# Encoder layer with two attention branches: the banded branch scheduled two pairs per round

## The reference, cut to what matters

```python
def window_attention(q, k, v, rel_bias, sink):       # 8 query heads, 2 key heads, blocks of 128 queries
    logits = einsum(q_block, keys of the block and its two neighbours)
    logits = where(|i - j| <= 128 and inside, logits + bias, -1e30)
    m = maximum(max(logits), sink)
    p = exp(logits - m)
    p = p / (sum(p) + exp(sink - m))
    return einsum(p, v)
...
merged = sigmoid(ga) * oa + sigmoid(gb) * ob
x = x + gt1 * (merged @ w_out)
h2 = rms_norm(x) * (1 + sc2) + sh2
x = x + gt2 * expert_choice_moe(h2)                   # 16 experts, the larger part of the time
```

## Time and profile before

| | us |
|---|---|
| median of 3 runs | 2331.76 |
| lowest and highest | 2330.65, 2332.59 |
| the profiled execution: its own time | 2333.09 |
| the span of its profile | 2331.3 |
| TensorE busy | 2274.2 (98%) |
| VectorE busy | 1622.0 (70%) |
| ScalarE busy | 1223.5 (52%) |
| banded branch: first scores (item 40) to first product of the merge | 431.55 to 540.77 |

### The profile page before, as it was taken

The page is one execution under the profiler, slowest core; times in us unless marked ns, Lnnn a source line. Parts: engine busy times, 40 slices in busy tenths (PEclk is TensorE's granted clock), DMA queues, the critical chain, the costliest instruction groups (busy, mean ns, idle before and its releaser), DMA issues.

```text
span 2331.3 us, 55130 instructions
## 1 busy us (share of the span) xinstructions
PE 2274.2 (98%) x24018; PEld 1663.7 (71%) x24018; DVE 1622.0 (70%) x1977; ACT 1223.5 (52%) x1568; POOL 1089.1 (47%) x707
## 2 busy tenths in 40 slices
PE   7998999999999999989999999999999999999997
PEld 3554677664444458788888888888888888888874
DVE  4776666483222456878887878788878878887875
ACT  4233666583111245457556555665566555665654
POOL 0000111133323214656666677667666766766752
PEclk9999999999999999989999999999999999999998
DMA  9101201503222345578899999989998999999896
GB/s 339 35 28 70 58 2 38 182 2 91 55 55 62 101 146 165 185 271 319 303 333 343 314 335 334 324 314 343 331 320 319 344 331 311 340 334 320 322 326 251
DMA packets 252439, 524.24 MB, mean 225 GB/s; under 512 B 8411, under 2 KB 57676, under 8 KB 252076
## 3 DMA queue, kind: packets, MB, share of 16 engines
q1 hardware_dynamic: 241692, 488.51, 59.4%
q0 software_dynamic: 10512, 32.25, 4.8%
HBM read 492.42 MB, written 28.31 MB: 223 GB/s over the span
## 4 chain that ended last, share of the span: by engine, by line
PE 90%; DVE 3%; ACT 2%; DMA 2%; issue 1%; SPq 1%; POOL 0%; DVEq 0%; POOLq 0%; ACTq 0%
PE ps L1870 24%; PE ps L1871 24%; PE ps L1872 24%; PE ps L2265 4%; PE ps L2054 3%; PE ps L2066 3%; PE ps L1931 3%; PE ps L1966 1%; DMA arena<-w_in 1%; PE ps L2004 1%; ACT arena L1085 1%; PE ps L1907 1%; PE ps L2238 1%; PE ps L1956 1%; PE ps L2202 1%
## 5 line engine op out<-in xcount | busy, mean ns | idle before, releaser
L1870 PE MATMUL ps<-arena 128*128 128x160 bf16 (+4 forms) x5624 | 1391.9, 267 | 6.9 <-issue 2.7
L1871 PE MATMUL ps<-arena 128*128 128x160 bf16 (+4 forms) x5624 | 1392.5, 267 | 0.0
L1872 PE MATMUL ps<-arena 128*128 128x160 bf16 (+4 forms) x5624 | 1392.4, 267 | 0.0
L1392 DVE TENSOR_TENSOR arena<-arena 128x2048 bf16<-128x2048 f32 x379 | 912.1, 2411 | 217.9 <-ACT arena L972 212.7
L972 ACT ACTIVATE arena<-arena 128x2048 bf16<-128x2048 f32 x384 | 727.0, 1905 | 217.9 <-PE ps L1872 176.2
L1870 PEld LDWEIGHTS ps<-arena 128*128 128x128 bf16 x5624 | 550.2, 98 | 157.6 <-issue 18.3
L1872 PEld LDWEIGHTS ps<-arena 128*128 128x128 bf16 x5624 | 550.2, 98 | 152.3
L1871 PEld LDWEIGHTS ps<-arena 128*128 128x128 bf16 x5624 | 550.2, 98 | 140.6 <-issue 0.3
L868 POOL TENSOR_TENSOR arena<-arena 128x320 bf16<-128x320 f32 x128 | 260.3, 2034 | 10.0
L865 POOL TENSOR_TENSOR arena<-arena,ones 128x320 bf16<-128x320 f32 x128 | 193.2, 1510 | 138.9 <-DVE arena L1735 138.6
L1243 ACT ACTIVATE arena<-ps 128x160 f32<-128x160 f32 x256 | 77.6, 303 | 299.8 <-PE ps L1872 299.8
(11 more groups left out here) (267 smaller groups left out, 2211.1 us busy)
## 6 DMA issues: line engine op xcount, KB each, us to landing
arena<-w_e_gate SPq DMA_DIRECT2D x64, 2048.0 KB, 8.9
arena<-w_e_up SPq DMA_DIRECT2D x64, 2048.0 KB, 9.8
arena<-w_e_down SPq DMA_DIRECT2D x64, 2048.0 KB, 9.3
arena<-w_ada SPq DMA_DIRECT2D x12, 2048.0 KB, 9.2
arena<-w_in SPq DMA_DIRECT2D x30, 512.0 KB, 5.2
arena<-x_sample SPq DMA_DIRECT2D x16, 512.0 KB, 3.8
arena<-w_in SPq DMA_DIRECT2D x3, 2048.0 KB, 17.3
arena<-w_out SPq DMA_DIRECT2D x2, 2048.0 KB, 8.6
```

What stands on the lines that cost most here:

```text
L1392: ve.tensor_tensor(lo, stage_half(kind, a), hi, ALU.subtract).then_inc(lo_done, 1)
L1870: pe.matmul(out, w_hi, x_hi, start=start, stop=False)
L1871: pe.matmul(out, w_hi, x_lo, start=False, stop=False)
L1872: return pe.matmul(out, w_lo, x_hi, start=False, stop=stop)
```

## The change

```diff
--- before.py
+++ after.py
@@ -121,12 +121,10 @@
         r = [("OT", pv // NPAIR)] if pv % NPAIR == NPAIR - 1 else []
         return r + [("PV", pv)]
 
-    for i in range(len(items) + 4):
+    for i in range(first_b):
         if i == 0:
             s.append(("NA", NT - 1))
-        if i == first_b:
-            s.append(("Z",))
-        lag = 1 if i <= first_b and (i == first_b or wide[i]) else 2
+        lag = 1 if wide[i] else 2
         while t < i - lag and t < len(items):
             s += [("T", t, n) for n in range(2)] + [("TE", t, n) for n in range(2)]
             t += 1
@@ -134,17 +132,15 @@
                 s += values()
                 pv += 1
         parts = []
-        if t < len(items) and t <= i - lag:
+        if t <= i - lag:
             parts = [("T", t, n) for n in range(n_parts(items[t]))]
             t += 1
         copies = [("TE",) + x[1:] for x in parts]
-        done = i - (4 if i <= first_b + 4 else 5)
-        if done >= 0 and done % NPAIR == 0 and done < len(items) and (done < first_b) == (i <= first_b + 4):
-            s.append(("RB", done // NPAIR))
+        if i >= 4 and i % NPAIR == 0:
+            s.append(("RB", i // NPAIR - 1))
         early = 2 if len(parts) == 4 else 0
         s += parts[:early] + copies[:early]
-        if i < len(items):
-            s += [("S", i), ("MX", i)]
+        s += [("S", i), ("MX", i)]
         if i in (1, 3):
             s.append(("NB" if i == 1 else "NC", NT - 1))
         if i == 5:
@@ -154,12 +150,8 @@
             s_ac += 1
         s += parts[early:3]
         s += copies[early:3] if early else copies
-        v = values() if pv < len(items) and pv <= (t - 2 if parts else t - 1) else []
-        if v and items[pv][0] == 1:
-            s += v[:-1]
-            v = v[-1:]
-        if i < len(items):
-            s.append(("EX", i))
+        v = values() if pv <= (t - 2 if parts else t - 1) else []
+        s.append(("EX", i))
         if v:
             s += v
             pv += 1
@@ -171,7 +163,50 @@
         if i >= first_b - 6 and i % 2 == 0 and c < 12:
             s.append(("AR", c))
             c += 1
-        if i == len(items) + 1:
+
+    def turned(i):
+
+        r = []
+        for n in range(n_parts(items[i])):
+            r += [("T", i, n), ("TE", i, n)]
+        return r
+
+    for i in range(first_b, len(items) + 4, 2):
+        if i == first_b:
+            s.append(("Z",))
+            s += [("T", t, 0), ("T", t, 1), ("TE", t, 0), ("TE", t, 1)]
+        if i % NPAIR == 0 and i <= len(items):
+            s.append(("RB", i // NPAIR - 1))
+        if i < len(items):
+            s += [("S", i), ("MX", i), ("S", i + 1), ("MX", i + 1)]
+        if s_ac < c:
+            s.append(("AC", s_ac))
+            s_ac += 1
+        if i == first_b:
+            s += [("T", t, 2), ("TE", t, 2), ("T", t, 3), ("TE", t, 3)]
+            t += 1
+        if i < len(items):
+            s += [("EX", i), ("EX", i + 1)]
+        if i <= first_b + 2:
+            s += values()
+            pv += 1
+        else:
+            s += [("PV", i - 4), ("PV", i - 3)]
+            pv = i - 2
+        for g in range(pv // NPAIR):
+            if g not in normed:
+                s.append(("NM", g))
+                normed.add(g)
+        for k in (i - 2, i - 1):
+            if first_b <= k < len(items):
+                s += turned(k)
+                t = k + 1
+        if i % NPAIR == 0 and first_b < i <= len(items):
+            s.append(("OT", i // NPAIR - 1))
+        if i < len(items) and c < 12:
+            s.append(("AR", c))
+            c += 1
+        if i == len(items):
             s.append(("WS", 0))
     assert t == len(items) and pv == len(items) and len(normed) == len(items) // NPAIR and s_ac == 12
     for m in range(KD):
@@ -418,7 +453,6 @@
         g_done, g_free = sem("g_done"), [sem(f"g_free{n}") for n in range(5)]
         q_in, q_sqrt, qf_ready, q_high = sem("q_in"), sem("q_sqrt"), sem("qf_ready"), sem("q_high")
         s_done, nm_ready, e_done = sem("s_done"), sem("nm_ready"), sem("e_done")
-        b_done = sem("b_done")
         pv_done, o_norm, o_split = sem("pv_done"), sem("o_norm"), sem("o_split")
         rinv_ready, rb_ready, rb_copied = sem("rinv_ready"), sem("rb_ready"), sem("rb_copied")
         dg_ready, gt_ready = sem("dg_ready"), sem("gt_ready")
@@ -543,7 +577,7 @@
             return (n // 2, 4 * (n % 2)) if n_parts(items[i]) == 4 else (n, 0)
 
         def piece_vec(i, n):
-            return len(items[i][3]) > 4 and piece(i, n)[0] == 0
+            return (len(items[i][3]) > 4 or items[i][0] == 1) and piece(i, n)[0] == 0
 
         def narrow(i):
             return items[i][0] == 0 and len(items[i][3]) <= 4
@@ -559,9 +593,6 @@
 
         def rb_of(g):
             return rb[NPAIR * g >= first_b]
-
-
-        n_add = lambda i: i - first_b + 1
 
 
         block = ctx.enter_context(nc.Block())
@@ -1082,7 +1113,7 @@
                                 src = ps[:, 2 * hh + i % 2, 0:w]
                         else:
                             p_ = src = PbB[:, i % 4, hh, slice(*window(i)[1])]
-                        ac.activation(p_, src, ACT.Exp, bias=nm[:, i % 4, hh:hh + 1],
+                        ac.activation(p_, src, ACT.Exp, scale=1.0 if br == 0 else -1.0, bias=nm[:, i % 4, hh:hh + 1],
                                       accum_out=den[:, i // NPAIR % 3, 2 * j + hh:2 * j + hh + 1]).then_inc(e_done, 1)
                 if k == "TE" and not piece_vec(*s[1:]):
                     i, n = s[1:]
@@ -1533,19 +1564,21 @@
                         ve.wait_ge(t_done, job_at[(("T", old, n_parts(items[old]) - 1), 0)] + 1)
                         ve.wait_ge(s_done, 2 * i + 2)
                         cols = slice(*window(i)[1])
-                        p_ = PbB[:, i % 4, :, cols]
-                        both = biasm.rearrange("p (v j) n -> p v j n", v=2)[:, :, j, cols]
-                        ve.tensor_tensor(p_, ps[:, 2 * (i % 2):2 * (i % 2) + 2, cols], both, ALU.add).then_inc(b_done, 1)
-                        ve.wait_ge(b_done, n_add(i))
-                        ve.tensor_reduce(nm[:, i % 4], p_, AX.X, ALU.max, negate=True).then_inc(nm_ready, 2)
+                        for hh in range(2):
+                            ve.tensor_tensor_reduce(out=PbB[:, i % 4, hh, cols], in0=ps[:, 2 * (i % 2) + hh, cols],
+                                                    in1=biasm[:, NPAIR * hh + j, cols], scale=-1.0, scalar=3e38,
+                                                    op0=ALU.add, op1=ALU.min, accum_out=nm[:, i % 4, hh:hh + 1])\
+                                .then_inc(nm_ready, 1)
                 if k == "TE" and piece_vec(*s[1:]):
                     i, n = s[1:]
                     hh, a = piece(i, n)
                     b, free = job(("T", i, n))
                     if i >= 2:
                         ve.wait_ge(pv_done, i - 1)
+                    if i == first_b:
+                        ve.wait_ge(o_split, first_b // NPAIR)
                     z = min(4, len(items[i][3]) - a)
-                    ve.tensor_copy(PTs[0][:, i % 2, hh, a:a + z, :], b[:, 0:z * P].rearrange("p (n q) -> p n q", n=z))\
+                    ve.tensor_copy(PTs[items[i][0]][:, i % 2, hh, a:a + z, :], b[:, 0:z * P].rearrange("p (n q) -> p n q", n=z))\
                         .then_inc(free, 1)
                 if k == "RB":
                     g = s[1]
@@ -2043,7 +2076,7 @@
                     else:
                         pe.wait_ge(z_done, 1)
                         if i >= first_b + 2:
-                            pe.wait_ge(b_done, n_add(i - 2))
+                            pe.wait_ge(nm_ready, 2 * i - 2)
                         scores(i, [ps[:, 2 * (i % 2) + hh, slice(*window(i)[0])] for hh in range(2)], k0, w, True)
                 if k == "T":
                     i, n = s[1:]
@@ -2087,7 +2120,7 @@
                     m, c = s[1], s[2]
                     n = 2 * m + c
                     if n == 0:
-                        pe.wait_ge(b_done, n_add(NI - 1))
+                        pe.wait_ge(nm_ready, 2 * NI)
                     if n == 1:
                         drained()
                         pe.wait_ge(o_norm, NI // NPAIR)
```

## The result

The changed kernel takes 2337.83 us (median of 16 runs, 2334.23 to 2341.76) against 2332.15 for the kernel before (16 runs on the same chip, 2328.53 to 2335.42): ratio 1.0025 [1.0019, 1.0032], 5.7 us slower. The forecast was 3.6 slower, so the direction was right and the size short by 2. The place was right in part: the forecast had most of the loss in the middle of the branch, and the largest part came at its start. The profiled execution of after took 2341.76, the slowest of its 16 and 3.9 above their median; that of before took 2333.09, 0.9 above its own median. So the trace of after may show somewhat more loss than a usual execution has.

The account below looks back on a forecast made before the run. TensorE, busy 98% of the span, was taken as the bound, with queue order making it wait; start +0.65, middle +2.4 and end +0.55 summed to +3.6 us: 2335.4 against the median, range 2329 to 2342, the forecast's own 2331 to 2338.

Parts of the forecast that it names:

- The changes of step: TensorE between scores, values and transposes: each costs 0.11 to 0.15; halving them saves 0.40 per round of two pairs.
- Rival 1: TensorE's changes of step decide and nobody is late: 8.42 per four three-tile pairs, time 2325; chance 0.09.
- The pitch x: VectorE's new per-head operation on 385 columns, start to start: 0.54 taken, near range 0.47 to 0.60, far end 0.95.
- The 0.07: Added to the 0.47 floor of VectorE's pitch for writing the kept result, between nothing and ScalarE's 0.10.
- Rivals 2 and 3: VectorE's operation longer than 0.63, time 2344, chance 0.24; or as long as the old two, time 2356, chance 0.06.
- rival 3: VectorE's operation does in one pass no more than the two did, pitch 0.95: time 2356; chance 0.06.
- The loop of a round: Banded rounds limited by queue order: 2.55 + 4x with NM, 4.49 + x with OT; 9.74 per four pairs, middle +2.4.
- Both named waits: TensorE idle before a round's fourth transpose job (NM rounds, for VectorE's copy) and before OT (for ScalarE's copy).
- the 9.6 of the sign: Sign in the profile after: scores of every second pair 9.6 to 9.9 apart per four pairs.
- The start: First banded scores (pair 40) to first three-tile scores (pair 52), including the entry from the global branch: +0.65.
- The standstill: At the entry TensorE's fourth transpose job waits for VectorE's copy until 446.1, the next chunk starting at 446.5 instead of 443.79.
- The end: From pair 76's scores to the merge's first product: 14.2, OT's copy standing before the first weight split on ScalarE; +0.55.

Follow-up runs that it names:

- x5: The changed kernel with the order of before (one pair per turn), keeping the new operation and the shared copies: ratio to before 0.9983, 2327.94 us.
- x13: After with NM behind VectorE's copies except the last, second pair's exponentials later, entry reordered, first weight split in parts: ratio to before 0.9982, 2327.42 us.
- x12: After with one more VectorE operation per round, a maximum nobody reads: 10.1 per four pairs against 9.54, 2343.74 us (one run).
- x6: After with NM moved behind VectorE's transpose copies: 9.32 per four pairs against 9.54, 2335.86 us (one run).
- x7: After with the exponentials of the round's second pair behind the first pair's transpose copies: 9.24 per four pairs against 9.54, 2338.52 us (one run).
- x4: After with all copies of banded tiles on ScalarE: 10.33 per four pairs against 9.54, ratio to before 1.0042, 2340.20 us.
- x1: After plus 56 small matmuls nobody reads, keeping TensorE busy at the entry: start 40.53 instead of 43.43, 2333.38 us (one run).
- x9: After with ScalarE's two pieces of the first weight split apart, the first before the last transposes: end 12.77 against 14.78, ratio to before 1.0012.
- x3: Before with only the new order, two pairs per round, old add, maximum and copies kept: ratio to before 1.0210, 2381.18 us.
- x8: After with global values and NM before scores 42 and the chunk product before the copies: start 37.78 against 43.43, ratio to before 1.0004.

## Why the prediction was right, and where it was short

**What bounds the kernel.** Right: what TensorE gained or lost in the branch arrived at the end, to within 2 us in each of the nine kernels with four or more runs. Not seen: TensorE was not quite full in the branch before. The stretch from 490 to 527 that I read the earlier trace rows is its best part; start, middle and end together have 4.5 us of idle TensorE, and the new operation alone takes most of it away and gains 4.3 us. The question "what would each part be worth without the others" was not asked, and its answer is the main finding: of the three parts one gains 4.3, one is worth nothing alone, and the order turns the gain into a loss of 5.7, which makes it cost about 10 (after against x5: 10.3 by the stretches, 9.8 by the ratios).

**The changes of step** went as predicted: 1.08 and 1.46 in a round. Rival 1 (2325, nobody late) fails for the reason given against it. The best order found, x13, has 9.01 where rival 1 had 8.42: T3 behind T0 and the copies in it remain.

**The operation.** The pitch x is 0.48, near the floor of my range of 0.47 to 0.60, not the 0.54 chosen. The accumulator read of 0.083 does come as an instruction of its own, as the Trainium skill says ("VectorE: DVE Perf Modes", Two Vector instructions with no wait between them), but it lies inside the overlap of two operations and adds nothing. The 0.07 came from ScalarE's kept sum, and that analogy was wrong. Rivals 2 and 3, longer operations, are out by a wide margin. (One argument against rival 3 misread its row: three operands take 0.743 on 512 columns, which is more than the add's 0.690 on 514, not less.) x12 shows what a longer VectorE queue costs: its 0.48 per round comes back as 0.47 in every second round and 0.10 in the others.

**The loop of a round** is the part that was most right. Formulas with x = 0.48: 4.47 and 4.97; measured 4.51 and 5.03. Twelve rounds of these make 57.2, and the middle took 57.16. With x = 0.48 the forecast's own sum would have given about +0.65 for the middle in place of +2.4; the rounds are 0.04 and 0.06 longer than the formulas, and over twelve of them that brings it back to the measured +1.28. That the one round hangs on VectorE's copy and the other on ScalarE's is shown by x12, x6, x7 and x4, each within 0.1 of what was expected for a round. Both named waits were there. Four pairs at 9.54 lie just under the 9.6 of the sign, again by x.

**The start** is the step that failed: +0.65 was said, +3.73 measured. The standstill was foreseen (chunk product 14.95 after the scores of pair 40 was the forecast, 15.13 the measurement). I treated its length as its whole price. Behind it the granted clock was 0.50, and chunk product and scores took 1.72 and 0.64 longer; x1 gives 2.90 for all of it and +0.83 for the rest. The Trainium skill ("TensorE: Matmul & The Clock Gate", HAM oscillation) warns of idle gaps that bring the slow clock back, and speaks of gaps somewhat longer than this one. This trace agrees on the effect, with 2.9 us of cost behind 3.06 us of idleness, and shows it for a shorter gap than the section names. I had read the 0.37 to 1.08 us gaps of before, all at clock 1.00, and had no row for a longer one.

**The end**: +0.55 said, +1.14 measured. The split starts 0.92 later after the scores of pair 76 than before instead of 0.56 (the forecast's 14.2 less 2.45), the rest of the way takes 2.67 instead of 2.45, and the wait for it is the one named (2.18, ended by VectorE's part). x9 removes it and gains 2.0, so the end was rightly located and half-sized. The product at 545.99 lies between 540 and 548.

Together: with x at 0.48 my own sum would have been +1.7 (between the +1.4 given for 0.47 and the +3.6 for 0.54), and the clock's 2.9 and the end's 0.6 bring it to 5.2. The three stretches have 6.15 and the medians 5.7; most of what is missing is the 0.6 of the middle. Two errors of opposite sign, 1.9 and 2.9 us, let the forecast look closer than its terms were, and that is luck. The forecast also called "within 0.2%" the likeliest outcome (0.52) and slower the less likely (0.38); slower came, by 0.25%, and 2337.83 lies at the upper edge of its own 2331 to 2338. Whether every timed execution of after has the slow clock in full can't be seen, since only one is profiled. Six other kernels with the same entry and no filler show it in the chunk product: 3.64, 3.64, 3.60, 3.43, 3.23 and 3.00 for x7, x9, x12, x6, x3 and x4. Without x3, whose start is long for other reasons too, their starts are 43.48, 43.42, 42.29, 41.66 and 41.20. So its length varies from one profiled execution to the next.

## What to carry to other kernels

Price each part of a bundle alone and in the order of before: here the cheap part carried the whole gain, and the reordering that it was bundled with spent it. When work is grouped into larger rounds on in-order engines, walk the loop from a step's first transpose through each engine's queue to the copy that frees its bank; the round can't be shorter than that, however idle the engines are on average, and moving one instruction (NM, or two exponentials) is worth as much as a faster operation (1.7 and 2.35 us in the middle, against the new operation's 1.35 in the old order). And a standstill of TensorE like the 3.06 us here is to be priced with the slow matmuls behind it, which cost up to as much again.

## What the hardware showed that I had not expected

- The granted clock fell to 0.50 after TensorE had stood still for 3.06 us, having been 1.00 in the busy stretch ahead. Chunk product and the scores behind it lost 1.1 us by it in x4 (standstill 2.99), 1.5 in x6, 1.6 in x3 (3.16), 1.7 in x12, and 2.4 in after, x7 and x9. Behind the wait before the first product the clock fell in after (2.18), x7 and x8 (1.96 both), 0.66 over the next 5 us, and in x3 (2.34), 0.69; it did not in x4 and x12 (2.17 both), x1 and x6 (1.96 both), 1.00 over the same 5 us. A gap of that length costs it in some executions only.
- 56 small bf16 matmuls of no use, 3.20 us of them, held the clock at 1.00 and delayed nothing.
- VectorE's combined operation reads 385 columns from PSUM and 385 from SBUF, writes 385 and keeps the minimum, in 0.555 us with a pitch of 0.48; an add of the same width without the minimum would be 0.558 by the earlier trace rows. Neither the second operator nor the kept minimum shows in its length.
